# Sums of squares of the latents taken by TensorE, product by product, in three feed-forwards of a two-layer backbone

## The reference, cut to what matters

```python
def rmsnorm(x, gain):
    y = xf * lax.rsqrt(jnp.mean(xf * xf, axis=-1, keepdims=True) + NORM_EPS)
    return (y * gain.astype(F32)).astype(x.dtype)

def pre(x, mod_j, gain):
    shift, scale, _ = mod_j
    return rmsnorm(x, gain) * (1 + scale) + shift

def ffn_sublayer(x, mod_j, g_pre, g_post, w_in, w_out):
    h = pre(x, mod_j, g_pre)
    return x + MACARON_W * mod_j[2] * rmsnorm(swiglu(h, w_in, w_out), g_post)
```

## Time and profile before

| | us |
|---|---|
| median of 3 executions | 2422.22 |
| lowest, highest | 2419.03, 2425.23 |
| the profiled execution | 2419.77 |
| its span in the trace | 2418.1 |
| TensorE busy, weight loads busy | 2314.3, 1946.4 |
| VectorE busy | 1278.7 |
| ScalarE busy | 555.1 |
| granted TensorE clock, mean share of full speed | 0.981 |

### The profile page before, as it was taken

How to read it: one execution, slowest core, us unless ns; L and a number is a source line. 1 busy time by engine, 2 the same in 40 slices (tenths; PEclk the granted TensorE clock), 3 DMA queues, 4 the chain that set the end, 5 groups by cost and what they waited for, 6 DMA issues and landing times.

```text
span 2418.1 us, 33655 instructions
## 1 busy us (share of the span) xinstructions
PE 2314.3 (96%) x13259; PEld 1946.4 (80%) x13259; DVE 1278.7 (53%) x2037; ACT 555.1 (23%) x1393; POOL 185.5 (8%) x252
## 2 busy tenths in 40 slices
PE   5999999999999999899999999999999999779998
PEld 3788899955556888788888998888899968458887
DVE  4377758564545777256765775676656421620001
ACT  3111111222233454341111113111111311621000
POOL 1100000001012332000000000000000000000000
PEclk8999999999999999999999999999999999989999
DMA  8555547622210000124545664355556432024462
GB/s 286 200 169 180 163 134 207 163 80 70 70 52 18 1 1 1 36 87 127 169 156 169 178 181 121 127 175 163 152 132 157 118 104 87 1 70 142 154 178 66
DMA packets 311464, 293.06 MB, mean 121 GB/s; under 512 B 6713, under 2 KB 292019, under 8 KB 311219
## 3 DMA queue, kind: packets, MB, share of 16 engines
q1 hardware_dynamic: 290611, 215.90, 30.0%
q0 software_dynamic: 20736, 75.51, 10.0%
HBM read 290.34 MB, written 1.05 MB: 121 GB/s over the span
## 4 chain that ended last, share of the span: by engine, by line
PE 90%; DVE 5%; ACT 2%; issue 1%; DMA 1%; SPq 0%; POOL 0%; DVEq 0%; POOLq 0%; ACTq 0%
PE bank L765 33%; PE bank L880 17%; PE bank L637 13%; PE bank L955 6%; PE bank L981 3%; PE bank L732 2%; PE bank L1279 2%; PE bank L1101 2%; PE bank L1112 1%; PE bank L1040 1%; DMA mring<-in_w_mod 1%; PE bank L1314 1%; PE bank L615 1%; DVE room L2324 1%; PE bank L1071 1%
## 5 line engine op out<-in xcount | busy, mean ns | idle before, releaser
L765 PE MATMUL bank<-hs,ring 128*128 128x256 f32 x1584 | 376.2, 382 | 1.3 <-ACT hs L1447 1.3
L765 PEld LDWEIGHTS bank<-hs,ring 128*128 128x128 f32 x1584 | 300.9, 191 | 48.6 <-issue 6.9
L880 PE MATMUL bank<-big,ring 128*128 128x128 f32 x2904 | 330.2, 275 | 0.0
L880 PEld LDWEIGHTS bank<-big,ring 128*128 128x128 f32 x2904 | 327.4, 192 | 0.2
L765 PE MATMUL bank<-room,big 128*128 128x256 f32 x1056 | 252.9, 383 | 0.0
L1896 DVE SCALAR_TENSOR_TENSOR mring<-mring,cond 128x1024 f32<-128x1024 f32 x196 | 240.2, 1278 | 7.8 <-DMA mring<-in_w_mod 7.8
L637 PE MATMUL bank<-hs,ring 128*128 128x512 f32 (+2 forms) x592 | 233.4, 548 | 0.0
L765 PEld LDWEIGHTS bank<-room,big 128*128 128x128 f32 x1056 | 201.9, 192 | 27.6
L637 PEld LDWEIGHTS bank<-hs,ring 128*128 128x128 f32 (+1 forms) x592 | 109.8, 188 | 105.9 <-issue 102.2
L517 POOL DMA_DIRECT2D mring<-in_w_mod x144 | 76.3, 530 | 1083.6 <-DVE mring L1890 498.4
L955 PE MATMUL bank<-hs,ring 128*128 128x256 f32 x704 | 153.8, 382 | 1.6 <-ACT hs L1447 1.6
(11 more groups left out here) (312 smaller groups left out, 3112.5 us busy)
## 6 DMA issues: line engine op xcount, KB each, us to landing
ring<-in_ffn_w_in SPq DMA_DIRECT2D x88, 1024.0 KB, 6.1
ring<-in_ffn_w_out SPq DMA_DIRECT2D x56, 1408.0 KB, 7.1
mring<-in_w_mod POOLq DMA_DIRECT2D x144, 512.0 KB, 3.9
ring<-in_gdn_w_in SPq DMA_DIRECT2D x16, 1024.0 KB, 5.6
ring<-in_diff_w_in SPq DMA_DIRECT2D x12, 1024.0 KB, 5.2
ring<-in_gdn_w_out SPq DMA_DIRECT2D x4, 1024.0 KB, 5.0
ring<-in_diff_w_out SPq DMA_DIRECT2D x4, 1024.0 KB, 5.1
cst<-in_consts SPq DMA_DIRECT2D x1, 1344.0 KB, 10.2
```

The source lines that it names most:

```text
L765: last = mm(bank[:, (g0 + b) % 4, 0:LAT], w[:, k, jj * P:(jj + 1) * P], rhs[:, k, :], start=start and k == 0, stop=(k == KC // 2 - 1), ski ...
L880: last = mm(bank[:, (go + b) % 4, 0:P], w[:, k, :], rhs[:, k, :], start=start and k == 0, stop=(k == FH - 1), skip_group_check=True)
```

## The change

For the three sums of `PE_SUMMED` (numbers 5, 7 and 10) VectorE's three additions are left out. ScalarE writes its four squares into four different buffers (`ssx`, the two of `xsq`, and the latents' half of `sq`), and so the fourth no longer waits for an addition. TensorE waits for the four squares one by one and adds them up itself: four calls for each square, sixteen in all, where there were four on the summed tile. All sixteen accumulate into the same two columns of bank 7. The other eight sums stay as they were; `summed_ahead_of` only recounts the semaphore.

```diff
+PE_SUMMED = [pre_event(2, 0), pre_event(3, 0), pre_event(5, 0)]
+
+def summed_ahead_of(p):
+
+    return 3 * sum(1 for e in range(p) if e not in PE_SUMMED)
...
+        def squares(p, jx):
+
+            if jx == 3 and p in PE_SUMMED:
+                return sq[:, :, side[0]]
+            return ssx if jx == 0 else xsq[jx % 2]
...
             def pre_sum(p):
 
-                pe.wait_ge(S["x_summed"], (p + 1) * 3)
                 pe.wait_ge(S["h_scaled"], p * 4)
+                if p in PE_SUMMED:
+                    for jx in range(4):
+                        pe.wait_ge(S["x_squared"], p * 4 + jx + 1)
+                        for t in range(2):
+                            for a in range(2):
+                                last = mm(bank[:, 7, t:t + 1], squares(p, jx)[:, a, t * P:(t + 1) * P], ones[:, 0:1],
+                                          start=(jx == 0 and t == 0 and a == 0), stop=(jx == 3 and a == 1), skip_group_check=True)
+                    last.then_inc(S["pre_sum"], 1)
+                    return
+                pe.wait_ge(S["x_summed"], summed_ahead_of(p + 1))
...
                     act.wait_ge(S["x_updated"], 4 * p + jx + 1)
-                    if jx == 3:
-                        act.wait_ge(S["x_summed"], p * 3 + 1)
-                    fn(ssx if jx == 0 else xsq[jx % 2], xs[:, 2 * jx:2 * jx + 2, side[v]], ACT.Square
+                    if jx == 3 and p not in PE_SUMMED:
+                        act.wait_ge(S["x_summed"], summed_ahead_of(p) + 1)
+                    fn(squares(p, jx), xs[:, 2 * jx:2 * jx + 2, side[v]], ACT.Square
                        ).then_inc(S["x_squared"], 1)
...
             def x_sums(p, js):
 
+                if p in PE_SUMMED:
+                    return
```

More of the change, by code:

```diff
@@ L1952, in x_sums @@
                     if jx > 1:
-                        dve.wait_ge(S["x_summed"], p * 3 + jx - 1)
+                        dve.wait_ge(S["x_summed"], summed_ahead_of(p) + jx - 1)
                     v_.tensor_tensor(ssx, ssx, xsq[jx % 2], ALU.add).then_inc(S["x_summed"], 1)
```

## The result

| | before | changed |
|---|---|---|
| median, us | 2419.92 (6 executions) | 2431.44 (6 executions) |
| lowest to highest | 2418.08 to 2425.23 | 2428.34 to 2433.74 |
| ratio, with its 95% interval | | 1.0041 (1.0031 to 1.0052) |
| the profiled execution, its span | 2419.77, 2418.1 | 2428.34, 2426.7 |

The changed kernel is slower by 0.41%, beyond the 0.3% that were set as the bound. By the interval that is 7.5 to 12.6 us, so its lower end lies only just beyond the bound; the forecast was +9.6 us and 2431.8 us. The ratio is not the quotient of the two medians: it stands for 9.9 us, and the medians lie 11.5 us apart.

A forecast was written before the change was run, and what follows sets the result against it. TensorE was taken to bound the kernel (busy 96% of the span, 90% of the last chain). 2 x 2.41 + 0.59 + 2 x 2.1 = +9.6 us on 2422.22 gave 2431.8 us, range 2425.0 to 2436.5.

The forecast's parts named there:

- TensorE's passes on the path at the second and third seam: Ahead of the second and third feed-forward, 32 passes replace 8 passes and 0.23 us of idling: +2.41 us each.
- The clock: Behind the one-column passes at the second and third feed-forward, the clock falls to half: +2.1 us each, bounds 0 to 3.5.
- The last seam: Ahead of the last feed-forward, 32 half-clock passes from the first square on end later than the old sum: +0.59 us.
- VectorE's and ScalarE's new order, and the wait: At the second and third feed-forward, VectorE's dropped additions save only 0.23 us of idling; added semaphore waits cost nothing.
- The sum: Whole kernel: two seams' passes, the last seam and two clock terms make +9.6 us, 2431.8 us.
- The clock that holds: Rival: one-column passes count as work, so no clock loss at the first two seams; +5.4, 2427.6 us; chance 0.28.
- The trickle that keeps the last seam's clock up: Rival: early passes hold the full clock ahead of the last feed-forward, -4.2 there; +0.6 in all, 2422.8 us; chance 0.07.
- The heavy case: Rival: second and third seam lose the whole clock price and some sum passes run at half; +13.8, 2436.0 us; chance 0.11.
- The 25 ns for a product of up to 64 columns: Rival: at all three seams a pass costs the table's 25 ns; -3.6 together, 2418.6 us; chance 0.04.

The follow-up runs named there:

- Experiment 4: Kernel before, VectorE's additions kept, the sum's four calls made four times over at the second and third feed-forward: 2428.24 us, ratio 1.0023.
- experiment 1: Changed kernel with the change only ahead of the second and third feed-forward, the last one's sum as before: 2429.05 us, ratio 1.0031.
- experiment 3: Changed kernel with 128 columns of ones as moving operand in place of one in the sixteen calls: 2423.88 us, ratio 1.0013.
- experiment 2: Changed kernel with the change only ahead of the last feed-forward, the other two sums as before: 2422.80 us, ratio 1.0006.
- experiment 5: Kernel before with only the fourth square given its own buffer at the three seams, so without its wait: 2422.70 us, ratio 1.0002.
- experiment 8: Kernel before with 128-column sums on TensorE ahead of the last feed-forward alone, plus products nobody reads in idle time at all three seams: 2414.68 us, ratio 0.9969.

## Why the prediction was right, point by point

- **TensorE's passes on the path at the second and third seam: +2.41 us each.** Right; 2.57 measured (3.46 - 0.89). TensorE was behind its own products there and not waiting for VectorE, so nothing was removed against what was added. Experiment 4 shows that the passes alone do it. The small error is the 0.23 us of idling that I took off: it was idle time of the weight loads alone, under the last product's end. In the chain the block begins 7.34 us behind the start of the 34 passes in both kernels, so the change won nothing back, and 24 passes at 0.107 us are the 2.57.
- **The clock: 2.1 us at each.** The mechanism was right, the term was mis-sized: 1.69 in both seams of the changed kernel and of experiment 1. My upper bound had all 14 passes and the spreading at half the clock; the clock came back before the spreading. The reason for a middle value, that the fall comes now earlier and now later or not at all, did not show: the 32 passes and the 14 together took 8.28 to 8.39 us in all six such seams (changed kernel, experiments 1 and 4). And the term stopped at the spreading: with what comes back behind the idle time it is 1.42 and 1.14 us (3.99 and 3.71 less 2.57). My reasoning, that a one-column pass looks like rest, was a guess from two stretches, both with idle time in them; experiment 3 shows that the fall goes with the columns, the only difference there. The page "TensorE: Matmul & The Clock Gate" of the Trainium skill, section "Part 1: The HAM clock gate", says that the clock goes by how busy the engine has been. The trace agrees only if busy doesn't mean what the busy column counts: that says 2.00 of 2.00 us for 1072 to 1074 with either kind of pass, and the clock fell behind the one and not behind the other.
- **The last seam: +0.59 us.** Right: +0.64, and 11.10 against 10.45 in experiment 2. It is the term with the least in common with what the change looks like: at half the clock TensorE cannot keep up with squares that come every 1.2 us, though the additions it replaces were on the path.
- **VectorE's and ScalarE's new order, and the wait: nothing.** Right; experiments 4 and 5.
- **The sum: +9.6.** The seams measure 9.17 in the profiles, 8.34 with what follows the first two; the rounds say 7.5 to 12.6. The nearness is in part luck: the passes were 0.16 us too low at each of two seams and the clock 0.4 too high, or 0.7 to 1.0 counted to the next pair. So is that of 2431.8 to the measured 2431.44: it was reckoned from 2422.22, the median of three executions, and that of six is 2419.92.
- **The rivals.** The clock that holds (2427.6) fell with the stretches above; with 128 columns it came true at the second and third seam. The trickle that keeps the last seam's clock up fell in the changed kernel; in experiment 8, with 128 columns and 128-column products ahead of the sum, the clock was up (1.00 over 2169 to 2172). The heavy case fell too: L698 ran at the full clock, and the half clock cost 1.69 us and not 3.5 and more. The 25 ns for a product of up to 64 columns in the table of the Trainium skill ("TensorE: Matmul & The Clock Gate", section "Back-to-back issue gap") fell as the price of a pass: 0.108 us here (3.46 / 32), and 0.112 with 128 columns (3.57 / 32), with the weight loads busy throughout. The prediction asked more of this table than the section gives it for: that is the gap of a single product in isolation, and of a stream of loads and products the section says that both set the spacing, as here. The loads of 186 ns and more, which I held against the table, overlap the products; the row that decides is their spacing of 0.110 us.

What stays open: why the clock is back sooner behind the idle time of the changed kernel, and the 0.86 us that it regains further on, ahead of the last seam. No run was made for either. Experiment 3 differs in the moving columns alone; what in them the granted clock answers to was not looked into.

## What to carry to other kernels

Before work is moved from an engine to TensorE, look at what TensorE does at that very place: where the chain lies on it already, an addition saved elsewhere is worth at most the idle time in the wait's bracket (0.23 us here, and in the end nothing), and each pass added costs its weight load in full. A reduction over partitions by one-column products is a poor use of the engine twice over: a pass costs as much as one with 128 columns, and behind a long block of them (32 here; behind 8 it held) the clock fell for the real products. Where the chain leaves TensorE for several us, products that nobody reads can pay for themselves, as long as they end before the next real one is due.

## What the runs showed of the hardware

- With a block of 32 one-column passes (3.46 us, PE and PEld busy throughout) the clock fell to half in all six seams of the changed kernel and of experiments 1 and 4, in five of them behind the block (14 passes in 4.82 us for 3.13) and once in its last passes (4.63 us). With 32 passes of 128 columns in the same place (3.57 us) it did not, in two seams (3.02 us).
- A float32 pass with 128 weight columns takes 0.11 us at the full clock and 0.21 at half, whether it has 1 or 128 moving columns.
- Filling two idle times of 5.2 us and one of 7 us with some 130 passes that nobody reads made the kernel 0.22% faster (0.13 to 0.31%).
